# Reordered mixer steps, packed setup product, earlier expert loads and a two-queue read-back in a one-core hybrid decoder trunk

## The chip, the core and the metric

The kernel runs on one core of one Trainium2 chip. A core has five engines, each with its own instruction stream: TensorE (PE in the rows, with its weight loads as PEld), VectorE (DVE), ScalarE (ACT), GpSimd (POOL) and SyncE (SP), and 16 DMA engines that serve transfers issued by any of them. Engines wait for one another through semaphores only. The metric is the device time of one execution in microseconds (us), median of several.

## The reference

One decoder layer over 16 learned meta tokens and 512 real tokens of width 1024, float32 throughout. In outline:

```
u = rmsnorm(h) ;  a_*, b_*, c_*, gate_logits = split(u @ w_in)          # 1024 x 8728
y_a = hgrn2(...)            # 4 heads, chunked gated linear attention, pairwise decays
y_b = gated_deltanet(...)   # 4 heads: causal conv of width 4 + silu on q, k, v; l2 norm; triangular solve; states
y_c = gla(...)              # 4 heads of 64 keys, decay from a rank-16 projection
merged = sum_n sigmoid(gate_n) * (y_n @ w_branch_n)
h  = h + merged @ w_out
u2 = rmsnorm(h)
h  = h + moe(u2)            # 4 groups x 8 experts, top-1 group, top-2 experts, hidden 256
out = rmsnorm(h)[real tokens]
```

The padding rows of the reference carry nothing; the kernel works on 528 tokens (16 + 512), with features on the partitions.

## The kernel before, in words

The program is five instruction streams written out by hand; the order of the code is the order on each engine. A helper gives every operation a name and a count on its stage's semaphore, and a consumer waits for "after(name)".

**Setup (L193 to L406).** The tokens are normed and turned (lines 382 and 389). Then one small product makes the 16 rows of the decay projection and the 8 rows of beta and decay logits: 8 steps of the contraction, each in two halves of 264 tokens, into 24 output rows (L399). ScalarE copies the result (L362), five small transposes turn it (L403, L405), and only then does TensorE begin the first column block.

**Mixers (L413 to L1587).** TensorE has two kinds of work. The filler are blocks of 128 columns of `w_in` (and later of `w_branch`): 8 contraction steps each, L729/L730 for a block over 528 tokens, L732 over 512, L723 for the merge. `fill(n)` issues n steps of it, `through(stage, seg, r)` all steps to the end of a block. The rest are the mixers' own small products, which wait for VectorE and ScalarE; the fillers stand between them. Stage a has 4 rounds (heads), stage b 4, stage c 2 (two heads at a time). A block may only be written to its PSUM bank once the bank's last reader is done (`wait_for_bank`, L672).

- A round of stage b on VectorE: convolve k (L1423, L1426), finish the head before it (L1316; in the first round the last a head, L1310, ahead of the convolution), take the decay differences `dif` and `min` (L1452, L1454, which need rows broadcast by a GpSimd DMA, `decay_rows`), silu of k (L1431, L1435), convolve q, then norm k (`kn`, L1459), and so on to `vr`, `QK` and the levels of the triangular inverse. ScalarE goes through the same order: exponentials of the decays `eg` and `E` (L1159, L1161), silu and square of k (`sk`, `kk`), root of the key norm (`lnk`, `rik`, L1167, L1169). TensorE sums the squares (`ssk`, L786) once `kk` is there. The gate block t0 goes to bank 1, which the convolution of v reads.
- A round of stage c has 7 levels l. VectorE at each level: difference, weighing (`za`, `zb`), copies of gate blocks at levels 0 and 1, the four chunk states at level 5 (L1302, L1305), and then the pick of the previous level's product (`P{l-1}`, L1272, L1273). TensorE's level product (L953) waits for `zb{l}` and `P{l-1}`.

**Out product and router (L1594 to L1861).** After the last merge VectorE makes 8 pairs `c{n}`, `h{n}`; TensorE waits for `h7` before the first of 8 out products (L1688, bank n each). SyncE reloads x and small tensors after `h7`, VectorE adds the residual (L1794), then norm, transposes, router logits, top-k and the token lists. The normed rows are stored to DRAM (`rows_kept`; the last by ScalarE's queue, L1665), and GpSimd fetches rows of a pair of experts by an indirect DMA (L1926).

**Experts (L1866 to L2188).** 32 experts, 3 MB of weights each (gate, up, down of 1 MB), in 6 sets of buffers. Sets 0 to 2 are loaded before the router, sets 3 and 4 once TensorE has finished the out product, set 5 after `rows_kept` and the last transpose of the router. Gate and up of expert e + 6 are loaded when the up product of e is done.

**End (L2285 to L2331).** The experts' results are read back from DRAM by 8 transfers of SyncE's queue; VectorE adds both results of a token tile (L2300), ScalarE takes the norm, VectorE multiplies (L2293), SyncE stores.

```
2295  for i in range(NT):
2296      v.wait_ge(sem(f"results_back{i}"), 32)
...
2302      if i:
2303          normed(i - 1)
2304  normed(NT - 1)
```

## Time and profile before

| | |
|---|---|
| median of 3 runs | 1180.84 us (1179.32 to 1184.23) |
| the profiled execution's own time | 1181.74 us |
| its span, first to last instruction | 1179.9 us |
| TensorE busy, granted clock | 1058.0 us (90%), 0.957 |
| VectorE, ScalarE, GpSimd busy | 477.3, 314.6, 58.5 us |
| moved by DMA | 174.35 MB, 148 GB/s on average |

TensorE is busy in 90% of the span, so its idle stretches and its clock are what to read first; up to about 822 us it is the only engine near its limit. From 32nd fortieth of the span on (944 us) the DMA engines move some 420 GB/s without a pause until the last expert. The two stages have different limits, and the numbers of the whole span are an average over them.

### The profile page before, as it was taken

The numbers are of one execution on the slowest core, as the hardware profiler recorded it, in microseconds if no ns is written. First come the engines' busy times: TensorE is split into PE (matmuls) and PEld (weight loads), VectorE is DVE, ScalarE is ACT, GpSimd is POOL, SyncE is SP. The second block draws the span as 40 slices with busy tenths as digits, with TensorE's granted clock in tenths as the row PEclk, the third lists the DMA queues.
The fourth block names the chain that finished last, engine by engine and source line by source line (L and its number), as shares of the span: only waits on it lengthen the run. The fifth ranks groups of instructions, "written<-read, shape, count | busy, mean of one in ns | idle before, by whom it ended". The sixth has DMA issues, their size and how long they took to land.

```text
span 1179.9 us, 15475 instructions
## 1 busy us (share of the span) xinstructions
PE 1058.0 (90%) x6440; PEld 641.1 (54%) x6440; DVE 477.3 (40%) x971; ACT 314.6 (27%) x602; POOL 58.5 (5%) x67
## 2 busy tenths in 40 slices
PE   7999999998999999999999899898993999887970
PEld 5666655664575575585556456443453556544440
DVE  3546364627337346247244443433124422111115
ACT  1625445324233324334323022110101011101012
POOL 0000000000000000000000000000000122212110
PEclk9999999999999999999999899998995899989895
DMA  9222222231132132131112111024808799999955
GB/s 294 67 54 68 58 55 63 63 76 49 43 74 57 37 76 54 37 76 54 48 42 72 40 50 55 1 101 176 317 36 341 292 419 420 420 420 423 421 241 223
DMA packets 111705, 174.35 MB, mean 148 GB/s; under 512 B 8947, under 2 KB 86988, under 8 KB 103314
## 3 DMA queue, kind: packets, MB, share of 16 engines
q1 hardware_dynamic: 98226, 132.77, 32.1%
q10 hardware_dynamic: 7680, 29.43, 6.2%
q0 software_dynamic: 5728, 11.14, 3.8%
q8 instruction: 52, 0.85, 0.3%
q14 instruction: 19, 0.16, 0.0%
HBM read 169.09 MB, written 12.60 MB: 154 GB/s over the span
## 4 chain that ended last, share of the span: by engine, by line
PE 74%; DMA 14%; DVE 9%; ACT 1%; issue 1%; SPq 0%; POOL 0%; DVEq 0%; POOLq 0%
PE ps L732 22%; DMA arena<-in_expert_w_up 11%; PE ps L729 8%; PE ps L723 7%; PE ps L730 7%; PE ps L1972 6%; PE ps L1688 5%; PE ps L777 2%; PE ps L1979 2%; DVE arena L1269 2%; PE ps L756 1%; PE ps L786 1%; PE ps L389 1%; DVE arena L1502 1%; DVE arena L1499 1%
## 5 line engine op out<-in xcount | busy, mean ns | idle before, releaser
L732 PE MATMUL ps<-arena 128*128 128x512 f32 x672 | 316.1, 606 | 6.6 <-DVE arena L1426 6.6
L732 PEld LDWEIGHTS ps<-arena 128*128 128x128 f32 x672 | 120.1, 191 | 122.4 <-issue 117.4
L729 PE MATMUL ps<-arena 128*128 128x264 f32 x416 | 128.5, 391 | 3.7 <-DVE arena L1426 2.9
L730 PE MATMUL ps<-arena 128*128 128x264 f32 x416 | 126.9, 387 | 0.0
L1972 PE MATMUL ps<-arena,gates 128*64 128x256 f32 x864 | 107.1, 404 | 17.2 <-DMA arena<-in_expert_w_up 15.8
L1269 DVE TENSOR_TENSOR arena<-arena 128x256 f32<-128x256 f32 (+6 forms) x194 | 91.5, 516 | 56.7 <-ACT arena L1090 35.4
L1972 PEld LDWEIGHTS ps<-arena,gates 128*64 128x64 f32 x864 | 65.0, 146 | 65.5 <-DMA arena<-in_expert_w_up 25.9
L723 PE MATMUL ps<-yT,arena 128*128 128x512 f32 x192 | 88.3, 616 | 2.2 <-DVE gates L1341 1.4
L729 PEld LDWEIGHTS ps<-arena 128*128 128x128 f32 x416 | 76.2, 191 | 19.6 <-issue 8.0
L730 PEld LDWEIGHTS ps<-arena 128*128 128x128 f32 x416 | 79.3, 191 | 13.7
L2127 DVE COPY gates<-ps 128x1024 f32<-128x1024 f32 x16 | 19.6, 1225 | 120.2 <-PE ps L1959 120.2
L723 PEld LDWEIGHTS ps<-yT,arena 128*128 128x128 f32 x192 | 37.1, 197 | 47.3 <-issue 46.8
L1688 PE MATMUL ps<-arena,gates 128*128 128x512 f32 x128 | 57.7, 608 | 5.5 <-DVE gates L1269 5.5
L777 PEld LDWEIGHTS ps<-arena 64*64 64x64 f32 x552 | 35.0, 134 | 31.6 <-DVE arena L1502 15.8
L2044 ACT ACTIVATE gates<-ps 128x128 f32<-128x128 f32 x32 | 8.9, 278 | 152.3 <-PE ps L1972 152.3
L1688 PEld LDWEIGHTS ps<-arena,gates 128*128 128x128 f32 x128 | 24.6, 196 | 35.6 <-issue 29.3
L777 PE MATMUL ps<-arena 64*64 64x64 f32 x552 | 40.5, 222 | 2.6 <-DVE arena L1502 2.4
L1979 PE MATMUL ps<-arena,gates 128*64 128x512 f32 x176 | 42.4, 604 | 0.0
L778 PE MATMUL ps<-arena 64*64 64x64 f32 x552 | 40.5, 222 | 0.0
L1926 POOL DMA_INDIRECT gates<-normed_tokens,gates x16 | 16.6, 1036 | 466.9 <-DVE rw L1770 392.1
L1273 DVE COPY_PREDICATED arena<-C,ps 128x512 f32<-128x512 int32 x56 | 39.5, 718 | 0.0
L2050 ACT ACTIVATE gates<-ps 128x512 f32<-128x512 f32 x32 | 19.1, 597 | 71.1 <-PE ps L1979 71.1
(327 smaller groups left out, 1265.2 us busy)
## 6 DMA issues: line engine op xcount, KB each, us to landing
arena<-in_w_in SPq DMA_DIRECT2D x68, 512.0 KB, 3.7
arena<-in_expert_w_gate SPq DMA_DIRECT2D x27, 1024.0 KB, 27.4
arena<-in_expert_w_up SPq DMA_DIRECT2D x27, 1024.0 KB, 31.9
arena<-in_expert_w_down ACTq DMA_DIRECT2D x18, 1024.0 KB, 33.2
arena<-in_w_branch SPq DMA_DIRECT2D x12, 512.0 KB, 3.8
C<-in_expert_w_gate SPq DMA_DIRECT2D x5, 1024.0 KB, 31.5
gates<-in_expert_w_up SPq DMA_DIRECT2D x5, 1024.0 KB, 36.2
arena<-in_w_out SPq DMA_DIRECT2D x1, 4096.0 KB, 13.9
```

Source lines behind the costliest of these rows:

```text
L723: mm = t.matmul(merge_bank[b], wt, rhs, start=first, stop=last)
L729: t.matmul(dst[:, 0:HALF], wt, uT[:, k, 0:HALF], start=(k == 0), stop=(k == KD - 1))
L730: mm = t.matmul(dst[:, HALF:], wt, uT[:, k, HALF:], start=(k == 0), stop=(k == KD - 1))
L732: mm = t.matmul(dst, wt, uT[:, k, META:], start=(k == 0), stop=(k == KD - 1))
L777: t.matmul(bank(n)[0:HP, at], lhs[0:HP, lo], rhs[0:HP, lo], start=True, stop=True)
L778: mm = t.matmul(bank(n + 1)[HP:, at], lhs[HP:, hi], rhs[HP:, hi], start=True, stop=True)
L1269: v.tensor_tensor(out_, a_, b2, op).then_inc(*q.did(name))
L1273: v.copy_predicated(tiles(pm), over(up(l).bitcast(I32), NT), tiles(src)).then_inc(*q.did(name))
L1688: mm = t.matmul(bank(n), gates[:, k, i * P:(i + 1) * P], wo[:, k, n % 2 * 512:(n % 2 + 1) * 512], start=(k == 0), stop=(k == KD - 1))
L1972: mm = t.matmul(dst, toks[:, k, :], src, start=(k == 0), stop=(k == KD - 1))
L1979: mm = t.matmul(bank(6 + b)[half * SLOTS:(half + 1) * SLOTS, :], hT[b][:, j * SLOTS:(j + 1) * SLOTS], weights[n][1][:, at:at + 512], start ...
L2127: v.tensor_copy(xT[q % 2], ps[:, 0:2 * 512].rearrange("p (k t) -> p k t", k=KD)).then_inc(pair_read.sem, 1)
```

## The change

It has eight parts; no transfer of weights and no arithmetic of the mixers is dropped.

1. The setup product is packed: each of 4 contraction steps writes 32 output rows of its own (`small_w` is padded from 24 to 32 columns, cleared by GpSimd before its load), in two rounds; the four partial sums are added by the products that turn the result (a 128 x 24 selection matrix `pick24` in place of the identity), and in stage c by a `gkw2` that holds the 16 rows four times.
2. Stage b, first round: VectorE convolves k before it finishes the last a head. All rounds: `dif`, `min` come after the convolution of q on VectorE, and `eg`, `E` after `kk` on ScalarE.
3. The b gate block t0 goes to bank 2 and waits for `q3` (before: bank 1 and `v3`); stage c's gate block waits for `v3`.
4. Stage c: the picks stand ahead of gate copies and states at each level; 3 of the 8 filler steps behind the first product stand ahead of it.
5. The first out product waits for `h{k}` step by step.
6. Gate and down of set 4 and gate of set 5 are loaded right behind sets 1 and 2; up of set 4 behind set 3; up and down of set 5 wait for the first pair's transposes (before: for the last router transpose), besides `rows_kept`.
7. The read-back is issued by SyncE (first results) and ScalarE (second results), with one semaphore per transfer.
8. The last tile is normed and stored in two column halves.

```diff
-            for k in range(KD):
+            for half in range(2):
                 for lo in (0, HALF):
-                    mm = t.matmul(wide(2)[0:24, lo:lo + HALF], small_w[:, k, :], uT[:, k, lo:lo + HALF],
-                                  start=(k == 0), stop=(k == KD - 1))
+                    for n in range(4):
+                        k = half * 4 + n
+                        mm = t.matmul(wide(2)[n * QUARTER:(n + 1) * QUARTER, lo:lo + HALF], small_w[:, k, :], uT[:, k, lo:lo + HALF],
+                                      start=(half == 0), stop=(half == 1))
...
-            t.transpose(bank(6, 24)[0:META], gkT[0:24, 0:META], ident[0:24, 0:24])
+            t.matmul(bank(6, 24)[0:META], gkT[:, 0:META], pick24, start=True, stop=True)
...
-              "b": {"k": wide(0), "q": wide(1), "v": wide(0), "g": real(1), "t0": real(0), "t1": real(1)},
+              "b": {"k": wide(0), "q": wide(1), "v": wide(0), "g": real(1), "t0": bank(2), "t1": real(1)},
...
                 through("c", "q", r)
+                fill(3)
                 t.wait_ge(*c_dve.after(f"q.{r}"))
...
-                fill(8)
+                fill(5)
...
                 def out_product(n, ks):
                     i = n // 2
                     for k in ks:
+                        if n == 0:
+                            t.wait_ge(*m_dve.after(f"h{k}"))
...
+                load_gate(sp, 4, 4)
+                load_down(sp, 4, 4)
+                load_gate(sp, 5, 5)
...
                 sp.wait_ge(sem("rows_kept"), 16 * NT)
-                sp.wait_ge(*pe2.after("T3b"))
-                load_weights(sp, 5, 5)
+                sp.wait_ge(*pair_turned.of(0))
+                load_second(sp, 5, 5)
+                load_down(sp, 5, 5)
...
+            def read_back(eng, k):
+                yv = y_dram.rearrange("(k i p a) c -> k i p (a c)", k=2, i=NT, a=2)
+                for i in range(NT):
+                    eng.dma_start(yg[2 * i + k], yv[k, i]).then_inc(sem(f"results_back{k}{i}"), 16)
...
             def fscalar(a):
+                a.wait_ge(sem("all_results"), 1)
+                read_back(a, 1)
...
+                for part, lo in (("l", 0), ("h", D // 2)):
+                    sp.wait_ge(*fdve.after(f"o{NT - 1}{part}"))
+                    sp.dma_start(ov[:, NT - 1, lo:lo + D // 2], h[:, NT - 1, lo:lo + D // 2]).then_inc(sem("stored"), 16)
```

VectorE at the start of stage b, before (L1310 finishes the last a head, L1423 and L1426 convolve k, the row that waits for decay_rows is `dif`):

```order
261 L1310 SCALAR_TENSOR_TENSOR arena<-ps,rowsT,arena 128x512 [waits a_act]
262 L1269 TENSOR_TENSOR yT<-arena 128x512 [waits a_dve]
263 L1445 MEMSET arena 128x3x112 [waits a_dve]
264 L1423 TENSOR_SCALAR arena<-ps,rowsT 128x528 [waits block_done]
265 L1426 SCALAR_TENSOR_TENSOR arena<-ps,rowsT,arena 128x527 [waits b_dve]
266 L1426 SCALAR_TENSOR_TENSOR arena<-ps,rowsT,arena 128x526 [waits b_dve]
267 L1426 SCALAR_TENSOR_TENSOR arena<-ps,rowsT,arena 128x525 [waits b_dve]
268 L1269 TENSOR_TENSOR arena<-arena,bcol 128x640 [waits decay_rows]
269 L1454 TENSOR_SCALAR arena<-arena 128x640 [waits b_dve]
270 L1431 SCALAR_TENSOR_TENSOR arena<-arena 128x528 [waits b_act]
```

The same place in the changed kernel (L1438 and L1441 convolve, L1325 finishes the a head):

```order
261 L1438 TENSOR_SCALAR arena<-ps,rowsT 128x528 [waits block_done]
262 L1441 SCALAR_TENSOR_TENSOR arena<-ps,rowsT,arena 128x527 [waits b_dve]
263 L1441 SCALAR_TENSOR_TENSOR arena<-ps,rowsT,arena 128x526 [waits b_dve]
264 L1441 SCALAR_TENSOR_TENSOR arena<-ps,rowsT,arena 128x525 [waits b_dve]
265 L1325 SCALAR_TENSOR_TENSOR arena<-ps,rowsT,arena 128x512 [waits a_act]
266 L1284 TENSOR_TENSOR yT<-arena 128x512 [waits a_dve]
267 L1465 MEMSET arena 128x3x112 [waits a_dve]
268 L1446 SCALAR_TENSOR_TENSOR arena<-arena 128x528 [waits b_act,b_dve]
...
274 L1441 SCALAR_TENSOR_TENSOR arena<-ps,rowsT,arena 128x525 [waits b_dve]
275 L1284 TENSOR_TENSOR arena<-arena,bcol 128x640 [waits decay_rows]
276 L1475 TENSOR_SCALAR arena<-arena 128x640 [waits b_dve]
```

The convolution of k went ahead of the head's end, and the two decay steps went behind the convolution of q.

VectorE in stage c, first round, levels 4 and 5, before (L1302 and L1305 are the states, L1272 and L1273 a pick, L1341 a merge step):

```order
612 L1269 TENSOR_TENSOR arena<-arena 128x8x32 [waits c_pe,c_act]
613 L1269 TENSOR_TENSOR arena<-arena 128x8x32
614 L1302 COPY arena<-ps 128x128 [waits c_pe]
615 L1305 SCALAR_TENSOR_TENSOR arena<-arena,ps 128x128 [waits c_dve] x3
616 L1272 COPY spare<-col 128x1 [waits c_dve,c_pe]
617 L1273 COPY_PREDICATED arena<-C,ps 128x512
618 L1272 COPY spare<-col 128x1 [waits c_dve,c_pe]
619 L1273 COPY_PREDICATED arena<-C,ps 128x512
620 L1341 TENSOR_TENSOR gates<-ps,gates 128x2x512 [waits block_done]
```

The same place in the changed kernel (L1317 and L1320 are the states, L1287 and L1288 a pick):

```order
611 L1284 TENSOR_TENSOR arena<-arena 128x8x32 [waits c_pe,c_act]
612 L1284 TENSOR_TENSOR arena<-arena 128x8x32
613 L1287 COPY spare<-col 128x1 [waits c_dve,c_pe]
614 L1288 COPY_PREDICATED arena<-C,ps 128x512
615 L1287 COPY spare<-col 128x1 [waits c_dve,c_pe]
616 L1288 COPY_PREDICATED arena<-C,ps 128x512
617 L1317 COPY arena<-ps 128x128 [waits c_pe]
618 L1320 SCALAR_TENSOR_TENSOR arena<-arena,ps 128x128 [waits c_dve] x3
619 L1356 TENSOR_TENSOR gates<-ps,gates 128x2x512 [waits block_done]
```

The two picks went ahead of the states.

## Rows read from the trace of the kernel before

**Rows 1.** The page's second part: GB/s in 40 slices of 29.5 us.
```profile
GB/s 294 67 54 68 58 55 63 63 76 49 43 74 57 37 76 54 37 76 54 48 42 72 40 50 55 1 101 176 317 36 341 292 419 420 420 420 423 421 241 223
```

**Rows 2.** Waits of TensorE: waiter <- awaited: us in total, times, longest.
```profile
PE ps L1959 <- DMA gates<-normed_tokens,gates: 12.8, 1, 12.8
PE ps L953 <- DVE arena L1273: 9.6, 4, 3.0
...
PE ps L732 <- DVE arena L1426: 6.6, 4, 1.8
...
PE ps L1688 <- DVE gates L1269: 5.5, 1, 5.5
PE ps L786 <- ACT arena L1165: 3.5, 1, 3.5
PE ps L938 <- DVE arena L1546: 3.1, 2, 1.8
PE ps L729 <- DVE arena L1426: 2.9, 1, 2.9
```

**Rows 3.** The chain in order of time: start us, us, what.
```profile
22.42 7.32 PE ps L399 x32
...
933.66 3.45 PE ps L1972 x32
```

**Rows 4.** Groups of TensorE's instructions: xcount | busy us, mean ns.
```profile
L953 PE MATMUL ps<-arena 64*64 64x64 f32 x384 | 9.2, 239 | 9.6 <-DVE arena L1273 9.6
```

**Rows 5.** Timeline, first round of stage b: start us, us, what [idle before it].
```profile
264.85 0.83 DVE L1269 TENSOR_TENSOR arena<-arena,bcol 128x640 f32<-128x640 f32 x1 [4.93 <-DMA arena<-token_rows]
...
273.14 0.83 DVE L1269 TENSOR_TENSOR arena<-arena 128x640 f32<-128x640 f32 x1 [1.74 <-ACT arena L1169]
...
290.44 0.69 DVE L1269 TENSOR_TENSOR arena<-ps,arena 128x512 f32<-128x512 f32 x1
...
292.78 0.27 PE L777 MATMUL ps<-arena 64*64 64x64 f32 x1
```

**Rows 6.** Timeline of ScalarE, second round of stage b, the root of the key norm.
```profile
357.41 0.79 ACT L1167 ACTIVATE arena<-ps,col 128x640 f32<-128x640 f32 x1 [2.85 <-PE ps L786]
```

**Rows 7.** Stage c as one stretch: busy us (x) by engine, PEclk, DMA share, GB/s.
```profile
600.00:790.00 190.00, 174.35 (x977) 98.84 (x976) 83.75 (x168) 41.59 (x87) 0.00 (x0) 0.96 0.15 41
```

**Rows 8.** Timeline of stage c, first round: a filler block, and the states.
```profile
654.67 7.13 PE L723 MATMUL ps<-yT,arena 128*128 128x512 f32 x16
...
663.02 0.29 DVE L1302 COPY arena<-ps 128x128 f32<-128x128 f32 x1 [6.12 <-PE ps L1016]
```

**Rows 9.** Timeline of the out product: TensorE's first three products, VectorE's first step.
```profile
822.06 22.65 PE L1688 MATMUL ps<-arena,gates 128*128 128x512 f32 x48 [5.49 <-DVE gates L1269]
...
836.03 0.46 DVE L1801 TENSOR_TENSOR gates<-gates,rowsT 128x288 f32<-128x288 f32 x1 [14.02 <-DMA gates<-in_router_expert_b]
```

**Rows 10.** DMA issues of 840 to 915 us: xcount, KB each, median us to landing.
```profile
normed_tokens<-gates SPq DMA_DIRECT2D x3, 512.0 KB, 2.6
...
normed_tokens<-gates ACTq DMA_DIRECT2D x1, 512.0 KB, 7.4
gates<-normed_tokens,gates POOLq DMA_INDIRECT x2, 8.5
```

**Rows 11.** DMA issues of 1140 to 1180 us.
```profile
expert_results<-gates POOLq DMA_INDIRECT x4, 3.2
```

**Rows 12.** Timeline between router and experts: the token lists, and the first fetch.
```profile
901.60 0.37 DVE L1770 TENSOR_SCALAR gates<-gates 64x16 int32<-64x16 int32 x2
...
905.86 1.07 POOL L1926 DMA_INDIRECT gates<-normed_tokens,gates  x1 [392.09 <-DVE rw L1770]
```

**Rows 13.** Timeline of the end: read-back, first addition, last norm.
```profile
1155.41 5.05 SPq L2324 DMA_DIRECT2D arena<-expert_results  x8
...
1160.86 2.60 DVE L2300 SCALAR_TENSOR_TENSOR yT<-arena,rw,yT 128x1024 f32<-128x1024 f32 x2 [14.02 <-DMA arena<-expert_results]
...
1175.64 1.28 DVE L2293 SCALAR_TENSOR_TENSOR yT<-yT,rw,gates 128x1024 f32<-128x1024 f32 x1 [0.58 <-ACT rw L2317]
```

More of the change, by code:

```diff
@@ L202, in hybrid_trunk @@
         ssq = col[:, 3:8]
-        small_w = w0.take(KD * 24).rearrange("p (k c) -> p k c", k=KD)
-        gkw2 = sb("gkw2", [16, 2 * P])
+        small_w = w0.take(KD * QUARTER).rearrange("p (k c) -> p k c", k=KD)
+        gkw2 = sb("gkw2", [P, 2 * P])
+        pick24 = C[:, K_SEL:K_SEL + 24]
         lbc = sb("lbc", [P, 16])
@@ L517, in hybrid_trunk @@
                                 each(r - 1, ["oo", "ln", "ri"] if r else []) +
-                                each(r, ["abk", "ek", "lk", "eg", "E", "sk", "kk", "lnk", "rik", "abq", "eq", "lq", "sq", "qq",
+                                each(r, ["abk", "ek", "lk", "sk", "kk", "eg", "E", "lnk", "rik", "abq", "eq", "lq", "sq", "qq",
                                          "N", "abv", "ev", "lv", "sv", "abg", "eg2", "lg", "Z1", "sg"] +
                                      [f"Z{l}" for l in LB[1:]] + ["nw"])] + each(B_R - 1, ["oo", "ln", "ri"]))
-        b_dve = Order("b_dve", each(0, ["pad"]) + [x for r in range(B_R) for x in
-                                each(r, ["k0", "k1", "k2", "k3"]) + each(r - 1, ["y1", "y"] if r else []) +
-                                each(r, ["dif", "min", "tk", "km", "kr", "q0", "q1", "q2", "q3", "kn", "kb", "Ei", "Es", "tq", "qm", "qr",
+        b_dve = Order("b_dve", [x for r in range(B_R) for x in
+                                each(r, ["k0", "k1", "k2", "k3"]) + (each(r - 1, ["y1", "y"]) if r else each(r, ["pad"])) +
+                                each(r, ["tk", "km", "kr", "q0", "q1", "q2", "q3", "dif", "min", "kn", "kb", "Ei", "Es", "tq", "qm", "qr",
                                          "U", "Ua", "Ub", "v0", "v1", "v2", "v3", "gc", "kbg", "kd", "Da", "Db", "tv", "vm", "vr", "qg", "QK",
@@ L685, in wait_for_bank @@
                     else:
-                        t.wait_ge(*b_dve.after(f"{ {'v': 'k3', 'g': 'q3', 't0': 'v3', 't1': 'gc'}[seg]}.{r}"))
+                        t.wait_ge(*b_dve.after(f"{ {'v': 'k3', 'g': 'q3', 't0': 'q3', 't1': 'gc'}[seg]}.{r}"))
                 elif stage == "c":
                     if seg[0] == "t":
-                        t.wait_ge(*gate_read("b", int(seg[1]) % 2, 2 * r + int(seg[1]) // 2))
+                        head, n = 2 * r + int(seg[1]) // 2, int(seg[1]) % 2
+                        t.wait_ge(*(gate_read("b", 1, head) if n else b_dve.after(f"v3.{head}")))
                     elif seg == "k":
@@ L1030, in gate_begin @@
                 a.wait_ge(*block_done(stage, f"t{n}", r))
-                a.activation(row, real(n % 2), ACT.Abs).then_inc(sem("gate_size"), 1)
+                a.activation(row, AT[stage][f"t{n}"], ACT.Abs).then_inc(sem("gate_size"), 1)
                 a.wait_ge(sem("gate_size"), g)
@@ L1157, in mixers_scalar @@
                 softplus(b_act, ("abk", "ek", "lk"), r, b_em[:, 0:TOK], b_kbg[:, 0:TOK])
+                a.wait_ge(*b_dve.after(f"tk.{r}"))
+                a.activation(b_em[:, 0:TOK], b_em[:, 0:TOK], ACT.Exp).then_inc(*b_act.did(f"sk.{r}"))
+                a.wait_ge(*b_dve.after(f"kr.{r}"))
+                a.activation(b_kb, b_kf, ACT.Square).then_inc(*b_act.did(f"kk.{r}"))
                 a.wait_ge(*b_dve.after(f"dif.{r}"))
@@ L1332, in gate_part @@
                 v.wait_ge(sem("gate_soft"), gate_no(stage, n, r))
-                v.scalar_tensor_tensor(row, real(n % 2), 0.0, row, ALU.min, ALU.subtract).then_inc(sem("gate_read"), 1)
+                v.scalar_tensor_tensor(row, AT[stage][f"t{n}"], 0.0, row, ALU.min, ALU.subtract).then_inc(sem("gate_read"), 1)
             def merged(n):
@@ L1449, in mixers_vector @@
                     b_finish(r - 1)
+                else:
+                    a_finish(A_R - 1)
+                    v.wait_ge(*a_dve.after(f"y.{A_R - 1}"))
+                    v.memset(padding(), 0.0).then_inc(*b_dve.did("pad.0"))
+                    v.wait_ge(*b_dve.after("pad.0"))
+                less("k", b_em[:, 0:TOK], ck, b_em[:, 0:TOK], r)
+                unit("k", b_kf, ck, b_em, r)
+                convolve("q", cq, wide(1), r)
+                v.wait_ge(sem("decay_rows"), 16 * r + 16)
+                if r:
                     v.wait_ge(*b_dve.after(f"y.{r - 1}"))
-                v.wait_ge(sem("decay_rows"), 16 * r + 16)
                 tt(b_dve, f"dif.{r}", t5(b_es), t5(b_gr), head_col(q_g, r), ALU.subtract)
@@ L1558, in mixers_vector @@
                             tt(c_dve, f"Pd_{s}.{r}", tiles(c_pm[s]), tiles(gram_bank(s)), over(ident, NT))
+                    if l:
+                        for s in range(CH):
+                            v.wait_ge(*c_pe.after(f"gr{l - 1}_{s}.{r}"))
+                            v.wait_ge(*c_dve.after((f"P{l - 2}" if l > 1 else "Pd") + f"_{s}.{r}"))
+                            pick(c_dve, f"P{l - 1}_{s}.{r}", c_pm[s], l - 1, gram_bank(s))
                     if l in (0, 1):
@@ L1571, in mixers_vector @@
                         states(c_dve, c_pe, c_st, c_dec, r)
-                    if l:
-                        for s in range(CH):
-                            v.wait_ge(*c_pe.after(f"gr{l - 1}_{s}.{r}"))
-                            v.wait_ge(*c_dve.after((f"P{l - 2}" if l > 1 else "Pd") + f"_{s}.{r}"))
-                            pick(c_dve, f"P{l - 1}_{s}.{r}", c_pm[s], l - 1, gram_bank(s))
                     if l >= 4:
@@ L1667, in tensor @@
             def tensor(t):
-                t.wait_ge(*m_dve.after(f"h{KD - 1}"))
                 t.wait_ge(sem("out_w"), 16)
```

76 lines of the change are left out of this document (40 added, 36 removed).

## The prediction

> **What bounds the kernel now.** I read the page's slices first, then TensorE's waits, then the timeline around each wait, and last the DMA issues near the router. The slices show two regimes. From slice 32 on the DMA engines move 420 GB/s without a break until the last expert [rows 1]: that stretch is bound by 26 experts' weights. It begins when the first up product frees the first buffer, at about 923 us, and since no buffer is free before that, whatever comes earlier shifts it as a whole. In front of it TensorE is the bound, at full pace but for the stalls in its list of waits [rows 2]. So each stall that goes ahead of the experts counts in full at the end, if nothing else is late at that point; inside the expert stream nothing is gained, because the bytes there are the same.
>
> **The change part by part.** Times are those of the profiled execution.
>
> Setup product. The 16 matmuls leave 32 records and take 7.32 us [rows 3], each with 24 of 128 output columns of the array in use. Four of them now write four different quarters. Do they run side by side? The expert products, in halves of 64, put 32 records of 256 columns into 3.45 us [rows 3], where 32 records of 264 columns one behind another take 7.32: two at a time. Stage c's level products use four quadrants: 384 records of 64 columns in 9.2 us, 24 ns each [rows 4], against 55 ns at the pace of the setup product (7.32/32 = 229 ns for 264 columns): more than two at a time. No row has four column quarters of the full depth. Bounds: nothing saved, or 5.5 (a quarter of 7.32 remains). The turning products become plain ones with two records each, 0.3 more. I take 5.0, nearer to rows 4. GpSimd's two clears delay the small load by some 1 us, hidden because TensorE comes to it at 22.4, long after.
>
> The Trainium skill (TensorEngine Tiling (Array Packing), Tiling Modes) gives four independent tiles for 128 x 32, and up to 4 times for at most 32 output columns (Overview); it also says that changing the mode drains the array. By the page 5.0 stands; by rows 3 alone, which show two tiles only, the term would be 3.4.
>
> Start of stage b. TensorE waits 2.9 us for the convolution of k (its bank is the one that v wants) and 3.5 us for the squares of k [rows 2]. With the convolution ahead of the a head's end it runs at 247 to 250 us, when its block is ready, and the first wait goes. The squares then need the head's end (256.5, unchanged) and the chain of three exponents or logs (2.1), VectorE (0.7), exponent (0.6), product (0.8), square (0.7): 261.6, while TensorE comes at 262.5. So both waits go, and the next thing late is the decay rows: they land at 264.85 [rows 5] as before, because their DMA waits for the same head's end. From there: `dif` and `min` 1.3, two exponentials 1.4 and then the root 1.5, since ScalarE now has them in that order, puts `kn` at 268.5 against 273.14 [rows 5], 4.6 earlier. Everything to `QK` on VectorE hangs on `kn`. Before, `QK` ended at 291.13 and the first level product began at 292.78 [rows 5], so VectorE had 1.65 to spare. Saved: 4.6 + 1.65 = 6.2 us. Bounds 4.6 and 7.
>
> Other rounds of stage b. With t0 in bank 2 the waits of L732 for v's convolution go: 6.6 us in four rounds [rows 2], of which the first round's 1.3 are in the term above, so 5.3 in three. But ScalarE's root of the key norm began at 357.41, right behind the sums [rows 6]. Now `eg` and `E` stand in front of it, and they wait for `dif` and `min`, which stand behind the convolution of q: that ends at 356.6, `min` at 357.9, `E` at 358.6. The root is 1.1 us late, and the same spare 1.65 swallows it: 0.5 a round, 1.6 in three. Bounds 0 and 5.3. I take 1.6.
>
> Stage c. L938 waits 3.1 us for `q`; the three filler steps (0.89 us each, from 7.13 for a block of eight [rows 8]) stand there now. L953 waits 9.6 us in four places for picks [rows 2]: 1.8 where the pick of level 0 stood behind a gate copy whose block had just ended, and 3.0 where picks stood behind the states, which begin at 663.02 when TensorE's state products are done [rows 8]. Moved ahead, the picks are ready 4 us before. What is late next: `zb5`, ready at 657, and at level 6 the picks behind the merge step, which have TensorE's 7.1 us filler as cover. So 12.7 us go. The stretch has a mean clock of 0.96 [rows 7]: 190 x 0.04 = 7.6 us lost at the lower of two levels (1.2 instead of 2.4 GHz), each time behind one of these stalls. Bounds of what returns: 0 and 7.6; I take 4.6, because short waits (`vc`, a merge) stay. Term 17.3.
>
> Out product. The first product can begin when TensorE's merge ends and take its steps as `h0` to `h7` come: four are there, and the other four come 1.3 us apart over 5.5 us, against 8 steps of 0.89. The wait of 5.5 goes [rows 2]. The 48 records took 22.65 us [rows 9] against 3 x 7.13 less overlaps, 20.9: 1.8 at the lower clock behind that stall. But the transposes need the residual, which waits for small loads that are still issued after `h7` and land at 836.0 [rows 9]: with 0.46 + 0.68 + 0.69 `h1` is there at 837.9, and TensorE, 7.3 early, would come at 837.4. Term 6.8; bounds 5 and 7.3.
>
> Expert loads. Before, 6.3 MB are issued at 886 and run at some 420 GB/s to 903; the last store of normed rows falls into them and takes 7.4 us, where three of the same size took 2.6 [rows 10]. Now 4.2 MB are left at that point, done at 898, since three loads went into the idle slice 29 [rows 1]. The store would land 4.8 earlier, but the lists are ready only at 901.97 [rows 12]: the fetch begins at 902.0 instead of 905.86, 3.9 us. Then 3 MB of set 5 ran beside the fetch, 8.5 us [rows 10]; up and down of set 5 now wait for its end. A quarter-megabyte indirect store on idle queues took 3.2 [rows 11], and a fetch of twice that adds 0.6 at 420 GB/s: about 4. Together 8.0; TensorE's wait of 12.8 [rows 2] is where it shows. Bounds 3.9 and 9.4. The moved loads stand ahead of three row stores on SyncE, for which nobody waits until the last of them; the 2 MB issued after the transposes take 5 us of the 7 until the stream begins.
>
> End. SyncE issues 8 reads in 5.05 us, and VectorE begins at 1160.86, with two tiles [rows 13]. Now it needs one, and the reads are issued by two queues. From there it is VectorE to the end, 16 us with one wait of 0.58 [rows 13]. I take 0.9 at the start and 0.6 for the half-size last store, 1.5; bounds -0.5 and 3. The Trainium skill (DMA: Bandwidth & Descriptors, Issuing engines are not separate DMA queues) says that a second issuing engine only saves issue time. By it the first part would be 0.3 and the term 0.9; no row shows two queues reading at once.
>
> Sum: 5.0 + 6.2 + 1.6 + 17.3 + 6.8 + 8.0 + 1.5 = 46.4. 1181.74 - 46.4 = 1135.3; the profiled execution stands 0.9 above the median of the runs. I forecast 1135.
>
> **Rivals.** (1) The stalls come back elsewhere: stage c's clock does not recover (4.6 less), the out product meets the small loads fully (1.8 less), the fetch keeps its 8.5 us (4.1 less), stage b's later roots cost what the bank gives (1.6 less, and 3 in the first round). 46.4 - 15.1 = 31.3: 1150. For it: every removed wait leaves a chain with under 2 us to spare. Against: the terms are independent. (2) The packing does nothing and neither does the second queue: 6.5 less, 1142. For it: no row with four column quarters. (3) All of the clock and all of the banks' 5.3 come back: 3.0 + 3.7 + 3 more: 1125. (4) Slower: the packed product keeps so little of the array moving in each step that the clock falls to the lower level at the start of stage a and stays there while the level products of 64 columns follow. Each us of TensorE's work at that level costs one more (7.13 for a block becomes 14). From 46 us of such work on the change loses; 60 us would give 1135 + 60 = 1195. Against: the quadrant products of stage c stand in a stretch whose mean clock is 0.96 [rows 7].
>
> **How the numbers follow.** Forecast, 1128 to 1146: 0.62. (1), 1146 to 1162: 0.18. (2), 1142, which lies in the forecast's range: 0.08. (3), below 1128: 0.07. (4): 0.03. No change in the time, the gains being eaten by something that I don't see: 0.02. What a measurement of this kernel can tell from no change is about 0.5%, 6 us; every case but the last two is beyond it. Faster 0.95, within 0.02, slower 0.03. The range is 1125 to 1152: it takes in (3)'s upper part, (2), and half of (1), and leaves out under 2 in 10.
>
> **What would show it.** In TensorE's waits of the changed kernel: L953, L1688 (its new line) and the wait of L732 for the convolution are under 1 us each; at the start of stage b a wait of about 1.3 for `kb` and of 1.5 for `vr` stands in place of 2.9 + 3.5. The setup product takes about 2 us, not 3.5 or 7. The store of the last rows lands in 2.6 to 3 us and the first fetch in 4. The mean clock of stage c is 0.98 or more. From the first expert to the last instruction the time is as before, less 1.5 us. I am wrong if the span from 30 us to the out product is shortened by less than 20 us (then the chains behind the removed waits were the bound), if the fetch still takes 8 us without loads beside it (then its time is its own), or if DMA has a pause inside the expert stream, which would say that the stream is bound by buffers and not by bytes.

## The result: 1139.5 us, and the profile after

The changed kernel takes 1139.47 us (median of four executions, three of them at 1138.34 to 1140.36), the kernel before beside it 1181.65. One execution each of the changed kernel (2724.66 us) and of two experiments below, x4 (2178.46) and x7 (3725.78), was in a slower state; the medians count it, the ratios leave it out. The ratio is 0.9639, 95% interval 0.9611 to 0.9668. The forecast was 1135 in a range of 1125 to 1152: right in sign and range, 4.5 us too low. The profiled execution takes 1138.34 us, with a span of 1136.5 against 1179.9: 43.4 us less.

TensorE's waits of the changed kernel (waiter <- awaited: us in total, times, longest) answer to [rows 2]:

```profile
PE ps L2001 <- DMA arena<-in_expert_w_up: 24.4, 12, 3.5
...
PE ps L2001 <- DMA gates<-in_expert_w_up: 6.5, 3, 2.8
...
PE ps L1988 <- DMA gates<-normed_tokens,gates: 5.1, 1, 5.1
PE ps L776 <- DVE arena L1284: 3.9, 4, 1.3
...
PE ps L791 <- DVE arena L1284: 1.5, 4, 0.4
PE ps L782 <- DVE arena L1480: 1.5, 1, 1.5
...
PE ps L1692 <- DVE yT L1813: 0.7, 1, 0.7
```

The waits for picks (before: L953), for the convolutions, for the squares, for `q` of stage c and for `h7` are gone. New are the small ones of stage b, for `vr` (L776), `QK` (L791) and `kb` (L782), and the 0.7 of the first residual transpose (L1692). The wait for the fetch fell from 12.8 to 5.1. But the first line grew: before, it was 15.8 us in 7 waits. With the second line (8.2 us before, 6.5 now), TensorE waits 30.9 us for up weights in the experts' stream, where it waited 24.0.

Next the timeline at several places: start us, us, what [idle before it]. The setup product, against 7.32 us in [rows 3], and the first step after it:

```profile
21.66 1.99 PE L412 MATMUL ps<-arena 128*32 128x264 f32 x32 [1.32 <-DVE arena L259]
...
25.45 0.69 PE L743 MATMUL ps<-arena 128*128 128x264 f32 x2
```

The start of stage b, against [rows 5]: `dif`, the two exponentials, the root, `kn`, and the first level product (before 264.85, 273.14 and 292.78 for `dif`, `kn` and the product):

```profile
259.49 0.82 DVE L1284 TENSOR_TENSOR arena<-arena,bcol 128x640 f32<-128x640 f32 x1 [0.80 <-DMA arena<-token_rows]
...
260.35 0.63 ACT L1178 ACTIVATE arena<-arena 128x512 f32<-128x512 f32 x1 [3.96 <-DVE arena L1284]
260.88 0.73 ACT L1180 ACTIVATE arena<-arena 128x640 f32<-128x640 f32 x1
261.52 0.78 ACT L1182 ACTIVATE arena<-ps,col 128x640 f32<-128x640 f32 x1
...
263.09 0.82 DVE L1284 TENSOR_TENSOR arena<-arena 128x640 f32<-128x640 f32 x1 [2.25 <-ACT arena L1184]
...
280.97 0.27 PE L791 MATMUL ps<-arena 64*64 64x64 f32 x1 [0.37 <-DVE arena L1284]
```

The out product, which now follows the merge without idle time, and its interruption by the residual transposes, against [rows 9]; then the lists, the first fetch and TensorE's turn of the fetched rows, against [rows 12]:

```profile
783.41 20.76 PE L1707 MATMUL ps<-arena,gates 128*128 128x512 f32 x48
...
804.89 1.09 PE L1692 MATMUL ps<-C,yT 128*128 128x128 f32 x8 [0.72 <-DVE yT L1813]
...
862.00 0.37 DVE L1789 TENSOR_SCALAR gates<-gates 64x16 int32<-64x16 int32 x2
...
863.32 1.07 POOL L1951 DMA_INDIRECT gates<-normed_tokens,gates  x1 [362.36 <-DVE gates L1789]
...
866.77 1.97 PE L1988 MATMUL ps<-C,gates 128*128 128x128 f32 x8 [5.12 <-DMA gates<-normed_tokens,gates]
```

Stage c as one stretch (columns as in [rows 7]): the granted clock, third number from the end, is 1.00, that is 2.4 GHz throughout, where it was 0.96.

```profile
590.00:760.00 170.00, 167.01 (x976) 95.82 (x975) 82.83 (x166) 39.58 (x84) 0.00 (x0) 1.00 0.17 50
```

The page's GB/s by slices (of 28.4 us), against [rows 1]: the idle slice in front of the router is filled to 366, and the plateau of the stream lies at 414 to 418, where it had been 419 to 423.

```profile
GB/s 287 90 64 66 57 57 56 56 80 73 39 63 72 38 65 70 39 65 70 38 37 75 56 56 57 1 160 165 366 143 240 408 414 416 416 418 414 418 200 231
```

The last up product of the stream, before and then after; and the read-back after, against [rows 13]:

```profile
1140.45 3.67 PE L1972 MATMUL ps<-arena,gates 128*64 128x256 f32 x32 [2.13 <-DMA arena<-in_expert_w_up]
```

```profile
1096.71 5.18 PE L2001 MATMUL ps<-arena,gates 128*64 128x256 f32 x32 [2.98 <-DMA arena<-in_expert_w_up]
...
1113.24 2.27 ACTq L2340 DMA_DIRECT2D arena<-expert_results  x4
1113.27 2.12 SPq L2340 DMA_DIRECT2D arena<-expert_results  x4
...
1118.04 5.26 DVE L2330 SCALAR_TENSOR_TENSOR yT<-arena,rw,yT 128x1024 f32<-128x1024 f32 x4 [13.42 <-DMA arena<-expert_results]
```

The rows that the table below takes its ends from, and that don't stand above, are these, first of the kernel before (first block, stage c's first product, merge, transposes in the out product, turn of the first pair), then of the changed one (stage c's first product, merge):

```profile
30.77 0.71 PE L729 MATMUL ps<-arena 128*128 128x264 f32 x2
...
610.40 1.16 PE L938 MATMUL ps<-arena 64*128 64x128 f32 x16 [1.27 <-DVE arena L1546]
...
788.87 27.70 PE L723 MATMUL ps<-yT,arena 128*128 128x512 f32 x64 [1.41 <-DVE gates L1341]
...
844.55 1.04 PE L1675 MATMUL ps<-C,yT 128*128 128x128 f32 x8
...
914.01 1.97 PE L1959 MATMUL ps<-C,gates 128*128 128x128 f32 x8 [12.76 <-DMA gates<-normed_tokens,gates]
```

```profile
598.14 1.16 PE L952 MATMUL ps<-arena 64*128 64x128 f32 x16
...
755.87 27.71 PE L737 MATMUL ps<-yT,arena 128*128 128x512 f32 x64 [1.41 <-DVE gates L1356]
```

Each term is the difference of two such rows, less what had been gained up to there:

| up to | before, after | gained in all | this term | forecast |
|---|---|---|---|---|
| first block | 30.77, 25.45 | 5.3 | 5.3 | 5.0 |
| first level product of stage b | 292.78, 280.97 | 11.8 | 6.5 | 6.2 |
| end of stage b | see below | 13.7 | 1.9 | 1.6 |
| merge behind stage c | 788.87, 755.87 | 33.0 | 19.3 | 17.3 |
| transposes in the out product | 844.55, 804.89 | 39.7 | 6.7 | 6.8 |
| turn of the first pair | 914.01, 866.77 | 47.2 | 7.6 | 8.0 |
| last up product | 1140.45, 1096.71 | 43.7 | -3.5 | 0 |
| end | 1179.9, 1136.5 | 43.4 | -0.3 | 1.5 |

(End of stage b: stage c's first product moved from 610.40 to 598.14, but before it stood behind a wait of 1.27, and now behind three filler steps of 0.89.) The last row holds 1.5 lost at the last expert (3.67 and 5.18 us above) and 1.2 gained behind it. Up to the experts the sum came out 2.3 us better than forecast (47.2 against 44.9); inside the stream, which I had taken as constant, 3.5 us were lost.

### The profile page after: what moved, and what is told of

Its sections match the earlier page's. It is cut to its first block, busy times and chain, and to the rows that moved or that the text cites. A ratio compares the mean times of both kernels' runs of the same rounds, so it can differ in the third digit from the quotient of the medians.

```text
span 1136.5 us, 15499 instructions
## 1 busy us (share of the span) xinstructions
PE 1040.1 (92%) x6445; PEld 630.8 (55%) x6445; DVE 476.9 (42%) x972; ACT 314.8 (28%) x602; POOL 59.0 (5%) x69
## 4 chain that ended last, share of the span: by engine, by line
PE 68%; DMA 14%; DVE 12%; ACT 3%; issue 2%; SPq 1%; POOL 0%; DVEq 0%; POOLq 0%
PE ps L746 21%; DMA arena<-in_expert_w_up 11%; PE ps L737 7%; PE ps L743 7%; PE ps L744 6%; PE ps L2001 6%; DVE arena L1284 4%; PE ps L1707 3%; PE ps L791 3%; PE ps L2008 2%; PE ps L770 1%; DVE arena L1441 1%; DVE yT L2330 1%; DVE arena L1520 1%; DVE arena L1517 1%
## 5 line engine op out<-in xcount | busy, mean ns | idle before, releaser
L737 PE MATMUL ps<-yT,arena 128*128 128x512 f32 x192 | 84.8, 596 | 2.2 <-DVE gates L1356 1.4
L791 PEld LDWEIGHTS ps<-arena 64*64 64x64 f32 x552 | 35.0, 134 | 33.4 <-DVE arena L1520 15.8
L791 PE MATMUL ps<-arena 64*64 64x64 f32 x552 | 40.5, 222 | 4.0 <-DVE arena L1520 2.4
L1288 DVE COPY_PREDICATED arena<-C,ps 128x512 f32<-128x512 int32 x56 | 39.6, 719 | 0.0
L2161 DVE TENSOR_TENSOR gates<-gates,ps 128x128 f32<-128x128 f32 x32 | 9.1, 283 | 72.5 <-ACT gates L2073 72.4
```

Source lines behind the costliest of these rows:

```text
L737: mm = t.matmul(merge_bank[b], wt, rhs, start=first, stop=last)
L791: t.matmul(bank(n)[0:HP, at], lhs[0:HP, lo], rhs[0:HP, lo], start=True, stop=True)
L1288: v.copy_predicated(tiles(pm), over(up(l).bitcast(I32), NT), tiles(src)).then_inc(*q.did(name))
```

## Experiments

Twelve kernels; "turn" is TensorE's transposing of the first fetched pair, "stream" the time from there to the last up product, and the rate that of 950 to 1080 us. Turn, stream and rate are of one profiled execution each, the median and the ratio of several. A ratio in an experiment is against the kernel before as it ran beside it.

| kernel | median us | ratio to before [95%] | turn | stream | GB/s |
|---|---|---|---|---|---|
| before | 1181.65 | 1 | 914.01 | 226.4 | 420 |
| changed | 1139.47 | 0.9639 [0.9611, 0.9668] | 866.77 | 229.9 | 417 |
| x1_no_loads | 1145.16 | 0.9685 [0.9664, 0.9707] | 874.81 | 228.7 | 416 |
| x2_only_c | 1164.03 | 0.9848 [0.9823, 0.9873] | 896.59 | 227.0 | 420 |
| x3_only_b | 1170.68 | 0.9907 [0.9881, 0.9933] | 902.86 | 226.6 | 420 |
| x4_only_pack | 1178.88 | 0.9972 [0.9948, 0.9996] | 907.74 | 228.3 | 416 |
| x6_only_loads | 1174.95 | 0.9948 [0.9928, 0.9969] | 903.40 | 228.9 | 420 |
| y1_before_shift32 | 1186.17 | 1.0041 [1.0018, 1.0063] | 907.92 | 229.0 | 416 |
| y2_after_shift128 | 1135.54 | 0.9607 [0.9580, 0.9634] | 866.50 | 226.9 | 421 |
| c1_early_set5 | 1140.38 | 0.9656 [0.9628, 0.9684] | 869.89 | 228.7 | 416 |
| c2_one_queue | 1137.33 | 0.9630 [0.9595, 0.9664] | 867.72 | 230.1 | 416 |
| x7_root_first | 1132.48 | 0.9576 [0.9546, 0.9605] | 862.19 | 230.6 | 416 |
| z1_root_shift | 1129.62 | 0.9564 [0.9537, 0.9591] | 861.38 | 227.1 | 419 |
| z2_all_512 | 1128.88 | 0.9563 [0.9536, 0.9589] | 862.09 | 226.5 | 421 |

### The parts one by one

**x2_only_c**: the kernel before with the orders of stage c alone.

```diff
+                    if l:
+                        for s in range(CH):
...
+                            pick(c_dve, f"P{l - 1}_{s}.{r}", c_pm[s], l - 1, gram_bank(s))
                     if l in (0, 1):
...
                 through("c", "q", r)
+                fill(3)
...
-                fill(8)
+                fill(5)
```

> The kernel before with part 4 alone (picks ahead in stage c, fill of 3 and 5). Theory: idle time (12.7) and clock both come back, 19.7 us as the changed kernel's trace has it: 1161, ratio 0.983, and the mean clock of stage c rises from 0.96 to 0.99 or more. Rival: the better clock of stage c in the changed kernel came from what goes before it; then only the idle time goes, 12.7 us: 1168, ratio 0.989, the clock at 0.96 to 0.97.

18.0 us by the ratio (15.0 to 20.9): idle time and clock both, as the theory had it; the rival's 12.7 lie outside. The clock of the stretch of [rows 7] in this kernel:

```profile
600.00:790.00 190.00, 187.00 (x1022) 104.42 (x1021) 89.14 (x175) 41.67 (x87) 0.00 (x0) 1.00 0.24 78
```

So the clock comes back by part 4 itself. How much that is worth depends on the execution: from stage c's first product to the merge the kernel before and the four kernels that share its stage c take 178.5, 174.1, 175.7, 177.8 and 175.6 us, while the changed kernel and the others with part 4 take 157.7 to 158.1. The trace of before that I had was the slowest of the five. Against their mean, 176.3, the term is 17.2, not 19.3: 2.1 us of the table's row are luck of that trace.

**x3_only_b**: the kernel before with parts 2 and 3 alone.

```diff
-              "b": {... "t0": real(0), ...},
+              "b": {... "t0": bank(2), ...},
...
+                less("k", b_em[:, 0:TOK], ck, b_em[:, 0:TOK], r)
+                unit("k", b_kf, ck, b_em, r)
+                convolve("q", cq, wide(1), r)
+                v.wait_ge(sem("decay_rows"), 16 * r + 16)
```

> The kernel before with parts 2 and 3 alone (order at stage b's start, exponentials of the decays behind the squares, banks of the gate blocks). Theory: 6.5 us in the first round and 0.5 in each of three others, 8 in all: 1172.8, ratio 0.9932. Rival: the first round alone, since the later rounds' chain behind the root holds them: 6.5, 1174.3; or all the bank's 5.3 too: 11.8, 1169.

By the trace 7.0 us at the first level product (285.83) and 8.4 at stage c's first product (601.96): the sum of 8 stands, and the three later rounds give 1.5. The ratio says 11.0, with 8 at the edge of its interval (7.9 to 14.1); The trace of x3 is 11.1 us shorter than that of before, and 2.9 of them lie between stage c's first product and the merge, which x3 does not touch.

**x4_only_pack**: the kernel before with the packed setup product alone.

```diff
-                    mm = t.matmul(wide(2)[0:24, lo:lo + HALF], small_w[:, k, :], ...
+                    mm = t.matmul(wide(2)[n * QUARTER:(n + 1) * QUARTER, lo:lo + HALF], small_w[:, k, :], ...
```

> The kernel before with part 1 alone (packed setup product). Theory: 5.3 us, all of it kept to the end, because TensorE is the bound from there on: 1175.5, ratio 0.9955. Rival: part of it is given back at the start of stage b, where the chains of the other engines (decay rows, root) set the time: 2 to 3 us, 1178 to 1179.

The first level product stands at 286.94, 5.8 us earlier, and the turn 6.3 earlier; nothing is given back at stage b. 1.2 of these us are no gain of the packing: the product begins at 21.25 us here, at 22.42 before. But only 3.3 us are left at the end by the ratio (0.5 to 6.1). The stream of this kernel is 1.9 longer, at 416 GB/s, as in the changed kernel. That pointed at the packing, which has nothing to do with the experts, except for one thing: its selector adds 32 columns to the table `C`, and every buffer behind `C` in SBUF moves by 128 bytes.

**x6_only_loads**: the kernel before with part 6 alone. **x1_no_loads**: the changed kernel without it.

```diff
                 for n in (1, 2):
                     load_weights(sp, n, n)
+                load_gate(sp, 4, 4)
+                load_down(sp, 4, 4)
+                load_gate(sp, 5, 5)
...
-                sp.wait_ge(*pe2.after("T3b"))
-                load_weights(sp, 5, 5)
+                sp.wait_ge(*pair_turned.of(0))
+                load_second(sp, 5, 5)
+                load_down(sp, 5, 5)
```

> The kernel before with part 6 alone (expert loads in other places). Theory: the first fetch 3.9 us earlier and 4.7 shorter, less up to 1 at the start; the stream as long as before at 420 GB/s: 1181.7 - 7.6 = 1174, ratio 0.9936. Rival: half of it comes back in the stream, because the stream then begins with 2 MB still under way: TensorE's waits for up weights grow by 3 us and more, 1177 to 1178.

> The changed kernel with the expert loads as before (part 6 undone). In the changed kernel the expert stream, from TensorE's turn of the first pair to the last up product, was 3.25 us longer than before (226.4 to 229.9 us), and TensorE's turn came 7.6 us earlier than the parts in front of it explain. Theory: the early loads give 7.6 us at the first fetch and cost nothing in the stream; its 3 us are run-to-run spread, so 1139.5 + 7.6 = 1147 and the stream stays at about 230. Rival: the loads only borrow; bytes that were moved while nobody waited (3 MB of set 5 beside the fetch) now stand at the stream's start, so the stream shortens to 226.5 again and the time is 1139.5 + 4.3 = 1144. The profile shows it: the fetch at 8 us in both cases, the stretch from the first turn to the last up product 226.5 or 230.

By the trace both lie between the theory and the rival. From the start of the out product to the turn, part 6 saves 7.4 us in x6 (84.6 against 92.0) and 7.3 in x1's comparison (83.4 against 90.7). In the stream 2.5 come back in x6 at the full 420 GB/s, and 1.3 in the other. By the ratios 6.1 (3.7 to 8.5) and 5.4 remain, the former within reach of theory and rival alike.

### The buffers' place

**y1_before_shift32** changes no instruction of the kernel before; **y2_after_shift128** is the changed kernel.

```diff
-K_ID, K_INC, K_STR, K_UP, K_LOW = 0, P, 2 * P, 3 * P, (3 + LEVELS) * P
+SHIFT = 32
+K_ID, K_INC, K_STR, K_UP, K_LOW = 0, P + SHIFT, 2 * P + SHIFT, 3 * P + SHIFT, (3 + LEVELS) * P + SHIFT
```

```diff
-K_INC = K_SEL + QUARTER
+K_INC = K_SEL + P
```

> The kernel before with 32 unused columns in its table of constants, so that all buffers behind them in SBUF begin 128 bytes later in each partition, as in the changed kernel. No instruction is changed. So far the expert stream ran at 419 to 420 GB/s in the kernel before and in the two kernels without the packing, and at 416 to 417 in the changed kernel and in the two with the packing. Theory: the new place of the buffers does it: 416 to 417 GB/s in the stream, the stretch from the turn of the first pair to the last up product 229 to 230 us instead of 226.4, and 3 us slower in all (ratio 1.0025). Rival: the packing's other effects (its loads, a code that is longer) do it, or chance: 420 GB/s and 226.4 us, ratio 1.000.

> The changed kernel with 96 more unused columns in the table, so that the buffers begin 512 bytes later than in the kernel before, at the same place within 512 bytes. Theory of the place: 420 GB/s again, the stream back at 226.4, 3 us faster than the changed kernel: 1136, ratio 0.961. Rival: no difference, 416 to 417 GB/s and a ratio of 0.964.

The rates of the page, first y1, then y2:

```profile
GB/s 287 75 54 72 55 55 68 59 76 54 37 76 55 37 76 55 37 77 54 50 41 73 54 36 55 1 155 175 265 51 342 309 417 416 416 416 417 416 245 224
```

```profile
GB/s 299 81 63 68 57 57 56 56 74 80 39 59 76 38 61 76 34 62 78 31 46 70 61 53 60 1 114 167 368 140 250 401 419 421 420 420 422 420 235 232
```

The theory of the place holds in both directions: 128 bytes make the kernel before slower by 0.41% (0.18 to 0.63) with its stream 2.6 us longer, and 384 more bytes take the loss out of the changed kernel, stream 3.0 shorter. By the ratios y2 is 3.8 us faster than the changed kernel, but the two intervals overlap; it is the rate that decides. The plateau in the page tells the two placements apart in every one of the kernels run.

Sorted by the two things that differ in the stream, its lengths are (us):

| | set 5's up and down before the first pair's turn | behind it |
|---|---|---|
| old place (z2: at 512) | before 226.4, x2 227.0, x3 226.6 | x6 228.9, y2 226.9, z1 227.1, z2 226.5 |
| new place | x1 228.7, x4 228.3, y1 229.0, c1 228.7 | changed 229.9, c2 230.1, x7 230.6 |

The place is worth about 2 us in the left column and about 3 in the right. The later loads cost about 1.5 at the new place; at the old one x6 alone shows a cost (2.1 over the mean of the three beside it), y2, z1 and z2 none clear of the spread.

### Fetch and read-back

**c1_early_set5**: the changed kernel, but up and down of set 5 are under way during the fetch.

```diff
-                sp.wait_ge(*pair_turned.of(0))
+                sp.wait_ge(*pe2.after("T3b"))
```

> The changed kernel with up and down of set 5 waiting for the router's last transpose again (as in the kernel before), instead of the first pair's turn; the three early loads stay. Theory: the fetch is slow because of 2 MB beside it: 7 to 8 us again instead of 3.45, the turn of the first pair 4 us later; but those 2 MB are no longer at the start of the stream, which becomes 1 to 2.5 us shorter, so 2 us slower in all than the changed kernel: ratio 0.966. Rival: the fetch takes 3.5 to 4 us beside 2 MB too (its length came from the store's or the lists' side): then 1 to 2 us faster, ratio 0.962.

```profile
863.71 1.07 POOL L1951 DMA_INDIRECT gates<-normed_tokens,gates  x1 [362.68 <-DVE gates L1789]
```

```profile
869.89 1.97 PE L1988 MATMUL ps<-C,gates 128*128 128x128 f32 x8 [7.85 <-DMA gates<-normed_tokens,gates]
```

From the fetch's issue to the turn it is 6.2 us with 2 MB beside it, 3.45 without, and 8.15 in the kernel before with 3 MB. The fetch is slow by what runs beside it, as forecast, though 6.2 is less than the 7 to 8 expected, and the turn is 3.1 later, not 4. The stream gets 1.3 back, and the whole is 2.0 us slower by the ratios: the theory's number, though the two intervals overlap.

**c2_one_queue**: the changed kernel, all 8 reads issued by SyncE, one semaphore each.

```diff
-                a.wait_ge(sem("all_results"), 1)
-                read_back(a, 1)
...
+                for i, k in ((i, k) for i in range(NT) for k in range(2)):
```

> The changed kernel with the 8 reads of the end all issued by SyncE again, one semaphore per transfer kept. The changed kernel's first addition begins 4.8 us after the first issue (before: 5.5). Theory: the semaphore per transfer gave this, not the queue: 4.8 again, VectorE never waits after it, and the time is the changed kernel's (ratio 0.964). Rival: the second queue gave it: 5.5, the second addition waits, 0.7 us and more later, as a shorter issue (2.2 against 5.05) brings the later transfers ahead.

```profile
1112.78 5.24 SPq L2340 DMA_DIRECT2D arena<-expert_results  x8
...
1115.96 1.28 DVE L2330 SCALAR_TENSOR_TENSOR yT<-arena,rw,yT 128x1024 f32<-128x1024 f32 x1 [11.76 <-DMA arena<-expert_results]
1119.70 3.95 DVE L2330 SCALAR_TENSOR_TENSOR yT<-arena,rw,yT 128x1024 f32<-128x1024 f32 x3 [2.46 <-DMA arena<-expert_results]
```

Neither said this. The first addition begins 3.2 us after the first issue, but the second waits 2.5 for its tile. From the first issue to the end it takes 24.1 us, against 23.3 in the changed kernel and 24.5 before: the second queue is worth 0.9, semaphores and column halves 0.4. The median shows no loss; 0.9 us is below what it can tell.

### A better order

**x7_root_first**: the changed kernel with ScalarE's root ahead of the decay exponentials. **z1_root_shift** has y2's columns too. **z2_all_512** puts `gates`, `yT`, and all weight buffers of `arena` on multiples of 512 bytes instead.

```diff
-["abk", "ek", "lk", "sk", "kk", "eg", "E", "lnk", "rik", "abq", ...
+["abk", "ek", "lk", "sk", "kk", "lnk", "rik", "eg", "E", "abq", ...
```

```diff
+        sb("filler", [P, 32])
         gates = sb("gates", [P, NB * KD, SEQ])
...
-        ARENA = 29500
+        ARENA = 29568
...
-            apart = arena[:, 2 * WX + 828:ARENA] ...
+            apart = arena[:, 2 * WX + 896:ARENA] ...
```

> The changed kernel with ScalarE's root of the key norm (lnk, rik) ahead of the exponentials of the decays (eg, E) in stage b. Theory: the root is no longer held by min: 1.4 to 2.8 us earlier in the first round and about 1.1 in each other; the waits of TensorE for kb (1.48), vr (4 in all, 3.9) and QK (1.5) shrink, 3 to 5 us faster than the changed kernel: 1135 to 1136.5. Rival: Ei and Es or the key's products, which need eg and E, become the chain, and it gives under 1 us.

> Both improvements together: the changed kernel with the root ahead of the decay exponentials (4.3 us in front of the experts by the trace of that run) and with 96 unused columns more, which put the buffers at their old place within 512 bytes (3.1 us of stream and 1.5 at the last expert). If they add: 1136.5 - 4.3 - 4.6 = 1127.6 of span, 1129 us, ratio 0.955. If the shift's gain depends on when the stream starts, it is 1132 again.

> The changed kernel with the root ahead, and the weight buffers in gates, yT and arena all at addresses that are multiples of 512 bytes (in the kernel before some were at 256 and some at 496 within 512). Theory: the nearer to such a multiple, the faster a transfer is written: over 421 GB/s in the stream, 225 us or less from the first turn to the last up product, faster than the other combination. Rival: what counts is only whether the place within 256 bytes is the old one: 420 GB/s, 226.5 us, the same time.

In x7's timeline the root stands before the exponentials, and `kn` (third row) comes at 262.02 instead of 263.09:

```profile
258.97 0.79 ACT L1178 ACTIVATE arena<-ps,col 128x640 f32<-128x640 f32 x1 [1.86 <-PE ps L800]
...
261.61 0.63 ACT L1182 ACTIVATE arena<-arena 128x512 f32<-128x512 f32 x1 [1.07 <-DVE arena L1284]
```

```profile
262.02 0.82 DVE L1284 TENSOR_TENSOR arena<-arena 128x640 f32<-128x640 f32 x1
```

The out product begins 4.3 us earlier than in the changed kernel (779.10), within the 3 to 5 expected; TensorE's waits for `vr` shrink from 3.9 to 1.2. Of the 4.3 us, 1.1 are there at the first level product (279.89) and 3.2 come in the three later rounds. The median is 7.0 lower, the span of the profiled execution 5.4: in that, the last up product ran at 2.4 GHz and gave 1.5. What the median has beyond it stays open. The two gains add: z1 and z2 take 1129.6 and 1128.9 us, and their intervals lie wholly below that of the changed kernel. Placing every buffer at 512 gives 0.6 us of stream over z1, within the spread of the medians: the rival stands, or nearly.

## Why the prediction was right, and where it was off

**The bound.** Stalls in front of the experts count in full: 47.2 us were gained up to the first pair, and 43.4 are left at the end. The claim that the tail is constant is the step that failed, though the time came out in the range. "From the first expert to the last instruction the time is as before, less 1.5 us" was wrong by 5.3: from the turn of the first pair to the end it took 265.9 us and takes 269.7. Three things showed. The buffers' place costs 2.6 (y1) to 3.0 (y2). The loads that were moved behind the turn cost 1.3 by c1 and x1 and 2.5 by x6, but y2, z1 and z2 have them too, and their streams are only 0.1 to 0.7 longer than that of the kernel before. So this cost is not a fixed one, it doesn't add to that of the place (y2 with these loads is within 0.4 us of the old stream), and why x6 differs from y2 stays open. I had written that 2 MB take 5 of the 7 us and left it there; the 10 us behind the first up product ran at 317 GB/s against 341, which fits that they share the start of the stream. And the last up product had the lower clock, 5.2 us instead of 3.7; this comes in some executions of kernels of either kind (x1, x4, x6, c1, z1 have it; x2, x3, y1, y2, x7, c2, z2 do not), so it belongs to no part. "The bytes there are the same" was nearly true (2 MB more are left at the turn) and not enough: bytes cost by where they land and, less clearly, by when they are issued.

**Setup product.** 5.3 against 5.0, in part by luck: the product itself saved 5.3, the turning steps behind it cost 0.75 more (0.3 had been worked out), and the rest is that the product began 0.76 earlier in this trace (21.66 against 22.42; kernels without the packing have it at 21.4 to 22.6). The change is worth 4.6. Four column quarters do run side by side: 1.99 us for 32 records, a factor of 3.7, and the rival with two tiles only (3.4 us) is out. The rule of the Trainium skill (TensorEngine Tiling (Array Packing), Overview) of up to 4 times is borne out by that number. The granted clock stayed at 1.00 (2.4 GHz) from there to the out product, so the slow rival did not happen.

**Stage b.** 6.5 against 6.2, and 1.9 against 1.6. The waits came where forecast and in size: `kb` 1.48 (about 1.3 said), `vr` 1.28 (1.5 said). The reason for the small gain of the later rounds, `eg` and `E` in front of the root, was tested by x7: turned round, 3.2 us more come out of the three later rounds. With the 1.9 that is 5.1, about all of the 5.3 that the banks' waits had held.

**Stage c.** 12.7 of idle time went, as L953's absence shows. The clock gave 6.6 in this pair of traces and 4.5 against the mean of five, with 4.6 forecast. So the forecast term, 17.3, agrees with the mean (17.2), and the table's 19.3 is high because the trace of before was a slow one of a quantity that varies by 4.4 us between executions.

**Out product.** 6.7 against 6.8; the new wait is 0.7, where 0.5 had been worked out.

**Expert loads.** 7.6 against 8.0. The fetch began 2.9 earlier, not 3.9, since GpSimd starts 0.95 us behind the lists (862.37, 863.32), which my sum had set to nothing; the fetch was shorter by 4.7, not 4.1. The two errors nearly cancel. The last store of normed rows landed in 2.8 us, against 7.4 before, as forecast.

**End.** 1.2 of 1.5. The reads are issued in 2.27 us instead of 5.24 with one queue (c2), and at the end 0.9 us of that is left: with one queue the first tile comes 1.6 us earlier after the first issue, but VectorE waits 2.5 for the second. The Trainium skill (DMA: Bandwidth & Descriptors, Issuing engines are not separate DMA queues) says that a second issuing engine saves issue time alone. The trace agrees in so far as 0.9 is less than the 3.0 us of issue time saved; the term worked out by that page, 0.9, and the forecast's 1.5 lie on either side of the 1.2 measured.

**Rivals.** Stalls that come back elsewhere (1150), packing without effect (1142), slower (1195) and no change did not happen. Of the third (1125), the clock of stage c came back, but not the banks' 5.3, which x7 gets. The kernel landed at 1139.5 for a reason that none of them named.

## To carry over

A table that grows by some columns moves every buffer behind it: look at the plateau of the DMA rate before and after any change to SBUF's layout, for 1% of a stream that is bound by bytes can eat the gain of a small edit. Before an order on an engine is changed to take a wait away, ask for each instruction that is put in front of a chain's head what it waits for itself. One trace gives a stall's idle time well, but not what the clock loses behind it: take that from several.

## What the runs showed of the hardware

- **Place in SBUF.** By the buffers' addresses, `gates`, `yT` and `arena` begin at a multiple of 256 bytes in the kernel before, and 128 bytes behind one in the changed kernel. The weights' stream has 420 GB/s in the first case and 416 to 417 in the second. The Trainium skill (DMA: Bandwidth & Descriptors, How a descriptor splits into AXI transactions) says of reads that a transaction starts at a multiple of 256 bytes, and that a descriptor off it pays for bytes it doesn't use; here it is the written side that moved, so its use here is a guess. I counted 32-byte beats by it for one partition of the 18 matrices in the six sets, with gate and up in one run of 8 KB and down in two of 4 KB (before, 9 matrices start at a multiple of 256, 8 at 240 bytes behind one and one at 128; after, 9 at 128, 8 at 112 and one at 0). That estimate gives 4692 beats before, 4700 after (0.2% more), and 4608 with all at 0 (1.8% fewer). The runs have 1% between the first two, and 0.3% between z1 and z2. So the direction agrees, the sizes do not, and the measurement decides; what the cost hangs on in detail was not shown.
- **The indirect fetch** of half a megabyte took 3.45 us from GpSimd's start to TensorE's turn with no loads beside it, 6.2 with 2 MB (c1) and 8.15 with 3 MB (before).
- **The clock.** Without its pick waits stage c had a granted clock of 1.00 (2.4 GHz) throughout in each of the nine kernels with part 4; with these waits, in five kernels, it was below that in one to four of nine stretches of 20 us (the lowest 0.83), and not in the same ones each time.
